# Rebuilding the last stage of a decoder block on one core: split gate weights and expert rows added in flight

## What is computed

```python
# 64 experts, 8 of them for each token; the shared expert is added to h earlier
h = h + sum over the token's 8 experts of weight * ((silu(xb @ w_gate[e]) * (xb @ w_up[e])) @ w_down[e])
h = h + (p @ w_ple) * sigmoid(rmsnorm(h, g_ple) @ w_ple_gate)     # p 512x256, w_ple 256x1024, w_ple_gate 1024x1024
out = rmsnorm(h, g_final)                                         # rmsnorm(x, g) = x * rsqrt(mean(x*x) + 1e-6) * g
```

## Time and profile before

| | |
|---|---|
| median of 3 runs | 1379.09 us (1377.03 to 1379.1) |
| the profiled execution's own time | 1374.77 us |
| its span on the core | 1373.1 us |
| PE busy over the span | 1276.9 us (93%) |
| DVE busy | 892.3 us (65%) |
| ACT busy | 580.4 us (42%) |
| POOL busy | 318.4 us (23%) |
| moved from and to HBM | 302.30 MB and 37.75 MB |

### The profile page before, as it was taken

How to read it: one execution, slowest core, us unless ns; L and a number is a source line. 1 busy time by engine, 2 the same in 40 slices (tenths; PEclk the granted TensorE clock), 3 DMA queues, 4 the chain that set the end, 5 groups by cost and what they waited for, 6 DMA issues and landing times. The chain is left out here.

```text
span 1373.1 us, 19307 instructions
## 1 busy us (share of the span) xinstructions
PE 1276.9 (93%) x6173; PEld 913.8 (67%) x6174; DVE 892.3 (65%) x1834; ACT 580.4 (42%) x943; POOL 318.4 (23%) x245
## 2 busy tenths in 40 slices
PE   4999999999999899859999999999999999997886
PEld 3777877667668795346777777777767777774333
DVE  5444244655556436667788787787887887882685
ACT  3232424343445201045655655656656556552211
POOL 5633243223224300012211221222122122211000
PEclk8999999999899999979999999999999999998799
DMA  8832122111124121279999999999999999985940
GB/s 251 228 73 57 38 62 63 46 47 48 31 55 141 29 101 53 77 281 334 359 351 357 369 359 365 357 351 363 354 357 365 364 369 360 357 314 182 426 193 31
DMA packets 123408, 306.14 MB, mean 223 GB/s; under 512 B 27328, under 2 KB 85344, under 8 KB 97632
## 3 DMA queue, kind: packets, MB, share of 16 engines
q1 hardware_dynamic: 104496, 271.38, 55.4%
q0 software_dynamic: 18864, 34.12, 6.5%
HBM read 302.30 MB, written 37.75 MB: 248 GB/s over the span
## 5 line engine op out<-in xcount | busy, mean ns | idle before, releaser
L1271 PE MATMUL bank<-sb_w_hl,sb_xgT_hl 128*128 128x512 f32 x1536 | 369.0, 396 | 6.6 <-DVE sb_xgT_hl L1405 6.6
L1271 PEld LDWEIGHTS bank<-sb_w_hl,sb_xgT_hl 128*128 128x128 f32 x1536 | 286.4, 190 | 64.1 <-DVE sb_xgT_hl L1405 6.8
L1284 PE MATMUL bank<-sb_y,sb_work 128*128 128x512 f32 x512 | 235.4, 602 | 0.9 <-ACT sb_work L1474 0.9
L195 PE MATMUL bank<-sb_x_hl,sb_w_hl 128*128 128x512 f32 x912 | 222.3, 400 | 0.0
L195 PEld LDWEIGHTS bank<-sb_x_hl,sb_w_hl 128*128 128x128 f32 x912 | 172.0, 192 | 46.4 <-issue 10.1
L1398 DVE TENSOR_TENSOR sb_w_hl<-sb_r,sb_w_hl 128x2048 fp32r<-128x2048 f32 x64 | 143.8, 2288 | 43.2 <-ACT sb_w_hl L1444 43.2
L1398 DVE TENSOR_TENSOR sb_w_hl<-sb_work,sb_w_hl 128x2048 fp32r<-128x2048 f32 x64 | 143.8, 2289 | 38.7 <-ACT sb_w_hl L1444 38.7
L1284 PEld LDWEIGHTS bank<-sb_y,sb_work 128*128 128x128 f32 x512 | 92.1, 190 | 93.0 <-issue 91.8
L869 POOL DMA_INDIRECT sb_r<-xn_rows,sb_work x66 | 68.7, 1041 | 357.2 <-PE bank L1263 276.6
L188 POOL TENSOR_TENSOR sb_w_hl<-sb_r,sb_w_hl 128x1024 fp32r<-128x1024 f32 x54 | 129.7, 2405 | 69.2 <-ACT sb_w_hl L1035 58.4
L735 ACT ACTIVATE sb_h<-sb_h,sb_small 128x31 f32<-128x31 f32 (+4 forms) x128 | 57.3, 495 | 207.9 <-DVE sb_small L642 139.2
(11 more groups left out here) (213 smaller groups left out, 1459.1 us busy)
## 6 DMA issues: line engine op xcount, KB each, us to landing
sb_y<-in_w_down SPq DMA_DIRECT2D x64, 1024.0 KB, 9.1
sb_r<-in_w_gate SPq DMA_DIRECT2D x32, 1024.0 KB, 6.9
sb_r<-in_w_up SPq DMA_DIRECT2D x32, 1024.0 KB, 8.4
sb_work<-in_w_gate SPq DMA_DIRECT2D x32, 1024.0 KB, 6.9
sb_work<-in_w_up SPq DMA_DIRECT2D x32, 1024.0 KB, 8.5
sb_r<-in_w_in SPq DMA_DIRECT2D x34, 512.0 KB, 3.9
sb_rows_even<-expert_rows SPq DMA_DIRECT2D x4, 2048.0 KB, 15.1
sb_rows_odd<-expert_rows SPq DMA_DIRECT2D x4, 2048.0 KB, 18.3
```

Of the source, the lines that this page charges most:

```text
L195: last = nc.tensor.matmul(out, w_hl[:, slot, zw, k, :], x_hl[:, zx, k, :], start=n == 0, stop=n == 3 * KD - 1)
L1271: last = nc.tensor.matmul(bank[BH][:, :], xgT_hl[:, zx, k, :], w[:, zw, :, k, :], start=n == 0, stop=n == 3 * KD - 1)
L1284: last = nc.tensor.matmul(bank[BO[i]][:, :], hT[:, c, :], wd[:, c, i * 512:(i + 1) * 512], start=c == 0, stop=c == 1)
```

## The change

The overflow block and the tail become one block. It does the following:

1. `w_ple_gate` is loaded in eight pieces of 512 KB during experts 52 to 59, one behind each expert's loads on SP's queue; for this the last twelve turns of SP's loop are written out. `g_ple` is loaded as a column per slice (`gcol`) and no longer as a broadcast row.
2. At the end of the expert block ACT scales each slice of the gate weight with the gain and rounds it (`scaled_gate_hi`), DVE forms the remainder (`scaled_gate_lo`): eight instructions of 128x1024 on each. The transposes of `p` and their two copies move there too.
3. SP loads only the first four rows of each token (2 MB per tile), into three buffers. POOL issues the second four rows as a transfer that adds them to what the buffer holds, when the first four have landed. DVE's adds are three per tile where there were six.
4. The gate product has three fp32r passes, 48 matmuls a tile. The tile is transposed unscaled, straight from `h`; ACT rounds it and DVE takes the remainder. The norm factor goes into the sigmoid's scale; ACT forms the sum of squares. The four gates have a buffer each.
5. DVE runs all four `finish` behind the last tile's remainder, and `scale_out(t-1)` behind `finish(t)`.

```diff
+                for e in range(NE - 12, NE - 2):
+                    next_gate_up(e + 2, e % 2)
+                    next_down(e, e % 2)
+                    k = e - NE + 12
+                    if k < KD:
+                        sp.dma_start(wgp[:, k], chunks(a["w_ple_gate"][0])[:, k]).then_inc(s_tail, 16)
...
                 run(dve, step)
+                dve.wait_ge(s_tail, 16 * KD)
+                for k in range(2):
+                    scaled_gate_lo(dve, k)
                 rows_out(NE - 1, 1, NE // 2 - 1)
+                for k in range(2, KD):
+                    scaled_gate_lo(dve, k)
...
+                all_rows_written(sp)
+                for t in range(NT):
+                    if t == 3:
+                        sp.wait_ge(T["added"], 1)
+                    sp.dma_start(row_at[t % 3], half_of_rows(t, 0)).then_inc(s_rows[t % 3], 16)
...
+                def add_other_half(t):
+                    pool.wait_ge(s_rows[t % 3], 16 * (t // 3) + 16)
+                    pool.dma_start(row_at[t % 3], half_of_rows(t, 1), accum_op=ALU.add, max_dma_last_dim=8192).then_inc(s_added_rows[t], 16)
...
+                    pe.wait_ge(T["xt_lo"], 2 * t + 2)
...
+                    for i in range(2):
+                        n = 0
+                        for k in range(KD):
+                            for zx, zw in PASSES:
+                                last = nc.tensor.matmul(bank[2 + 2 * (t % 2) + i][:, :], xnT_hl[:, zx, k, :],
+                                                        wg_hl[:, zw, k, i * 512:(i + 1) * 512], start=n == 0, stop=n == 3 * KD - 1)
+                                n += 1
+                        last.then_inc(T["gate_pe"], 1)
...
+                def round_rows(t):
+                    if t:
+                        act.wait_ge(T["gate_pe"], 2 * t)
+                    for i in range(2):
+                        act.wait_ge(T["xt_pe"], 2 * t + i + 1)
+                        nc.scalar.copy(xnT_hl[:, 0, 4 * i:4 * i + 4, :], psv(i, 4, P)).then_inc(T["xt_hi"], 1)
+                    squares(t, 0, 0, "ms")
...
+                round_rows(0)
+                for t in range(1, NT):
+                    gates(t - 1)
+                    round_rows(t)
+                gates(NT - 1)
...
+                def add_rows(t):
+                    rows = row_at[t % 3]
+                    dve.wait_ge(s_added_rows[t], 16)
...
+                add_rows(0)
+                for t in range(1, NT):
+                    add_rows(t)
+                    rest_of_rows(t - 1)
+                rest_of_rows(NT - 1)
+                dve.wait_ge(T["emb"], 8)
+                dve.wait_ge(s_gp, 16)
+                finish(0)
+                for t in range(1, NT):
+                    finish(t)
+                    scale_out(t - 1)
+                scale_out(NT - 1)
```

More of the change, by code:

```diff
@@ L1390, in _ @@
                 down(NE - 1, 1, NE // 2 - 1)
+                pe.wait_ge(s_p, 48)
+                pe.wait_ge(E["idx"], NE + NPAD - 1)
+                for c in range(2):
+                    for t in range(NT):
+                        last = nc.tensor.transpose(bank[(BL, 7)[c]][:, t * P:(t + 1) * P], prow[:, t, c * P:(c + 1) * P], ident)
+                    last.then_inc(T["p_tp"], 1)
             @block.vector
@@ L1531, in _ @@
                         pe.wait_ge(V["down"], 16 * j + 16)
-                        down_products(pe, Wd[0], V)
+                        down_products(pe, Wd_more, V)
                         pe.wait_ge(V["o_act"], j + 1)
+                pe.wait_ge(T["p_tc"], 2)
+                for t in range(NT):
+                    if t >= 2:
+                        pe.wait_ge(T["emb"], 2 * (t - 1))
+                    for i in range(2):
+                        for c in range(2):
+                            last = nc.tensor.matmul(bank[2 + 2 * (t % 2) + i][:, :], pTt[:, c, t * P:(t + 1) * P],
+                                                    wpl[c][:, i * 512:(i + 1) * 512], start=c == 0, stop=c == 1)
+                        last.then_inc(T["emb_pe"], 1)
@@ new lines, in _, with squares, gates @@
+            @block.scalar
+            def _(act):
+                more = act.value_load(ntot[0:1, 0:1], min_val=0, max_val=NOV)
+                with act.If(more > 0):
+                    with act.Fori(0, more) as j:
+                        act.wait_ge(V["gu"], j + 1)
+                        nc.scalar.activation(hid, bank[BH][:, 0:EH], ACT.Silu).then_inc(V["silu"], 1)
+                        act.wait_ge(V["hid"], j + 1)
+                all_rows_written(act)
+                for t in range(NT):
+                    for i in range(2):
+                        act.wait_ge(T["emb_pe"], 2 * t + i + 1)
+                        nc.scalar.copy(y[:, t, i * 512:(i + 1) * 512], bank[2 + 2 * (t % 2) + i][:, :]).then_inc(T["emb"], 1)
+                def squares(t, out, first, name):
+                    nc.scalar.activation(junk, h[:, t, :], ACT.Square, scale=D ** -0.5,
+                                         accum_out=part[:, first + t:first + t + 1]).then_inc(T[name], 1)
+                def round_rows(t):
+                    if t:
+                        act.wait_ge(T["gate_pe"], 2 * t)
+                    for i in range(2):
+                        act.wait_ge(T["xt_pe"], 2 * t + i + 1)
+                        nc.scalar.copy(xnT_hl[:, 0, 4 * i:4 * i + 4, :], psv(i, 4, P)).then_inc(T["xt_hi"], 1)
+                    squares(t, 0, 0, "ms")
+                def gates(t):
+                    act.wait_ge(T["rr"], t + 1)
+                    for i in range(2):
+                        act.wait_ge(T["gate_pe"], 2 * t + i + 1)
+                        nc.scalar.activation(sigs[t][:, i * 512:(i + 1) * 512], bank[2 + 2 * (t % 2) + i][:, :], ACT.Sigmoid,
+                                             scale=part[:, 4 + t:5 + t]).then_inc(T["sig"], 1)
+                round_rows(0)
[3 more added lines that the diff above has]
+                gates(NT - 1)
@@ L1560, in _ @@
                         dve.wait_ge(V["stored"], 16 * j + 16)
[L1562 to L1572, removed]
```

209 lines of the change are left out of this document (85 added, 124 removed).

## The result

The changed kernel takes 1399.65 us (median of 4 runs, 1395.83 to 1403.86), the kernel before 1379.09 us (1377.03 to 1379.3). The ratio is 1.0153, 95% interval 1.0122 to 1.0184: 20.6 us slower, where 11 us were forecast. The profiled execution took 1400.21 us with a span of 1398.4.

What follows compares the result with a forecast made beforehand. The tail was taken as bound first by a transfer, then by PE and DVE in turn. 1308.2 + 6.35 + 45.3 + 24.3 = 1384.1 against 1373.1, 11.0 us more, added to the median 1379.09: 1390 us, range 1375 to 1402.

Steps and rivals of the forecast that it cites:

- threefold cost: Rival for the tail's row transfers: adding costs three times a copy (15.6 us), time 1405; chance 0.13.
- 1, to SP's first row load: End of expert block: it ends later, so SP issues the first rows at about 1269.7, 2.9 us later.
- Link 2: Tail, loads until tile 1's rows are complete, at 1308.2, with 9.7 us per adding transfer, twice a plain one.
- 3, to tile 0's product: Tail, from tile 1's rows complete to the first gate product: three adds and two remainders, 6.35 us.
- Link 4: Tail, gate products: from the first product's start to tile 3's, 45.3 us, with hand-overs of 2.7 us.
- X: The start of tile 3's gate product in the tail, put 45.3 us after the first product's start.
- Link 5: Tail after tile 3's product starts: DVE's four finishes and four scalings end last, together 24.3 us.
- Waits for A2 and A3 don't bind: Tail: later tiles' row waits don't delay products; all eight transfers end by 1331.1, tile 2's product can start at 1345.8.
- the rival to which I gave 0.08: Expert stage: the cover for the extra gate weight loads fails, 3 to 7 us on top, 1393 to 1397; chance 0.08.
- Adding as fast as copying: Rival for the tail's row transfers: tile 1's rows complete at 1297.2, no change, 1379; chance 0.15.
- Served ahead of tile 2's plain load: Rival in the tail: POOL's transfers go first at a copy's rate, 4.8 us less, 1374; chance 0.14.
- A1: The time when tile 1's rows are complete in the tail, forecast at 1308.2.

Runs made afterwards that it cites:

- Experiment 1: The changed kernel with POOL's four row transfers copying and not adding, so the first four expert rows of each token are left out of the sum: 1382.57 us.
- Experiment 2: The changed kernel with the drain on POOL ahead of the root replaced by a wait on a semaphore: 1390.37 us.
- experiment 5: The kernel before with the gate weights loaded early in eight pieces, without the 4 MB load in the tail, nothing else changed: 1376.09 us.
- experiment 6: The changed kernel with the eight gate weight pieces behind every third expert from 36 on, not behind each from 52 on: 1398.28 us.
- experiment 8: The kernel of experiment 7 with the gate weight pieces spread as in experiment 6: 1367.14 us.
- experiment 9: The kernel of experiment 8 with tile 2's third half added earlier, the finishes of tiles 1 and 2 behind the last remainder, POOL's last output roots later: 1361.67 us.
- experiment 4: The changed kernel with the edits of Experiment 2 and experiment 3, and each tile's last steps put between the tiles' sums: 1380.4 us.
- experiment 7: The kernel of experiment 4 without adding transfers: SP loads all eight half tiles plainly and VectorE adds both halves: 1369.39 us.
- experiment 3: The changed kernel with VectorE forming each tile's remainder directly behind the sum of its rows: 1400.14 us.

## Why the prediction was right, and where its size was off

The direction and the mechanism hold: the adding transfers run at half rate and the tail gets longer for it. The size does not hold as well: 11.0 us were forecast and 20.6 measured. The median lies outside the 1384 to 1396 that the forecast gave "if its mechanism holds", and inside 1375 to 1402 because that range was stretched towards the threefold cost, which is not what happened. That much is luck. The chain's links, tail counted from the last group of 24 products (1244.26 before, 1253.51 after):

| link | predicted, us | measured, us | from |
|---|---|---|---|
| 1, to SP's first row load | 25.4 | 25.3 | 1253.51 to 1278.84 |
| 2, to tile 1's rows complete | 38.5 | 39.1 | to 1317.93, DVE's L1718 at 1317.95 |
| 3, to tile 0's product | 6.35 | 6.2 | to 1324.10 |
| 4, to tile 3's product, X | 45.3 | 50.5 | to 1374.64 |
| 5, to the end | 24.3 | 23.8 | to 1398.4 |
| tail | 139.9 | 144.9 | |

**Link 2** is right to 0.6 us with 9.7 us for an adding transfer. Experiment 1 shows that it is the adding. The sentence taken from the Trainium skill ("Collectives: The Full Stack", section "The bandwidth ceiling: the fold count and why AG ≠ RS ≠ AR") held for a transfer within one core as well: 215 GB/s against 426.

**Link 4** is the step that failed, by 5.2 us. The prediction said "Waits for A2 and A3 don't bind" and let the second sigmoid follow the product at once. It checked what DVE and PE wait for, and not that the sigmoid's scale comes from POOL, whose drain stands behind four adding transfers. The last row transfer did bind, by way of a root of 128 numbers. The prediction had its end nearly right (61.4 us after the first row load; measured 63.0, 1278.84 to 1341.8). Experiment 2 puts the cost at 7.4 us of tail. Without the drain the link is 43.1 us, 2.2 below the forecast: the three hand-overs take 2.57 us each, not 2.7, and the first product 13.0 and not 14.4. So an error in the other direction hid part of it.

**Link 5** is right: DVE's list ends last and has no gap of note.

```profile
1373.30 1.29 DVE L1727 TENSOR_TENSOR sb_xn3T_hl<-bank,sb_xn3T_hl 128x512 fp32r<-128x512 f32 x2 [12.47 <-ACT sb_xn3T_hl L1672]
...
1394.02 1.28 DVE L1742 SCALAR_TENSOR_TENSOR sb_h<-sb_h,sb_small,sb_r 128x1024 f32<-128x1024 f32 x1 [0.44 <-POOL sb_small L1595]
```

**The eight pieces**, which the prediction cost "at nothing", cost 3.8 us: the rival to which I gave 0.08. What failed is the size of the backlog, not the room. The room was 7.4 us for a down weight (before, issued at 1193.44 and used at 1209.94, 16.5 us later, with 9.1 to land), near the 7 of the prediction. The backlog was put at 4 to 5 us, and up to 3 for `gcol`. The down weight issued at 1198.95 landed 18.0 us later, so at the last expert it was 8.9 us. The demand of 413 GB/s (362 + 51) met 388 GB/s at a share of 1.00, which by my estimate alone is 2.0 MB, 5 us, over the 81 us. Experiments 5 and 6 show that the pieces cause it and that their density matters. Where the other 4 us come from, and why one wait of 0.7 to 1.4 us stays when the pieces are spread (0.89, 0.67 and 1.36 us in experiments 6, 8 and 9), I leave open. `gcol` was not taken away by itself in the changed kernel; in these three it is loaded sixteen experts earlier, and in experiment 5, which waits too, there is none.

**The rivals.** *Adding as fast as copying* and *threefold cost* are both excluded by the rates. *Served ahead of tile 2's plain load*: not seen, and A1 came 0.6 us late, not 16 us early. The sum of links and stage is 11.0 + 5.0 + 3.8 = 19.8 us, against 20.6 of the medians.

**What the change was worth in parts.** Early gate weights: some 2 us of gain (experiment 5, 0.15%). Adding transfers in place of plain loads, all else equal: 11 us of loss (experiments 4 and 7, 1380.4 and 1369.39). The drain: 9 us by the medians. The orders on DVE and POOL that experiment 4 mends on top of the drain: 10 us (1390.37 to 1380.4). Of that, experiment 3 alone shows nothing while the drain is there, so the two can't be valued apart. The twelve adds that DVE was spared (19 us of its time) were worth less than the transfers lost: with plain loads most of them lie beside PE's products and the transfers. Not all do: in experiment 7 the third and the fourth product start 5.0 and 4.8 us behind the end of the one before (1320.96 to 1325.97, 1338.60 to 1343.39), where the hand-over takes 2.6.

## What to carry to other kernels

Let a transfer add only where the transfer engines have time to spare: it costs them twice a copy, while the adds it saves may lie beside other work. Ask of every drain what else its engine has issued: on POOL, with a transfer in flight, it was a wait for that transfer, where a semaphore on the one result took 0.34 us. And when a stage gets a new engine order, follow the small operands too (a scale, a root), for they tie the path to an engine that looks idle.

## What the runs showed of the hardware that was not expected

- A drain on POOL held until the transfer in flight, POOL's own, had landed: 13.81 us for an adding one, 8.46 us for a plain one, with the root 0.3 us behind the landing each time (1341.8 and 1342.08, 1321.4 and 1321.71). With nothing in flight 0.15 us lie between the two instructions around it (1361.35 to 1361.51 in the changed kernel). With a semaphore in its place the root came 0.34 us behind the sum (1326.82 to 1327.16) while the transfer was in flight.
- An adding transfer from HBM into SBUF in fp32 moves 215 to 221 GB/s at a DMA share of 1.03 to 1.06; the same transfer as a copy 401 to 434 GB/s at 0.96 to 1.04 (experiment 1, 1297 to 1301).
- Near the full rate a little more load made loads land much later: with 413 GB/s wanted and 388 carried, a gate load's time to land went from 6.9 to 12.7 us, and the last down weight's from 9.1 to 18.0 us. It stays high with less: at 376 GB/s and a share of 0.97 in experiment 6 a gate load took 15.1 us, against 361 GB/s and 0.95 before.
- POOL's root over 128x1 takes 0.57 us where DVE is idle and 1.52 us in the three rows at the end of the tail that start 0.16 us behind a scaling of 1.28 us on DVE. DVE's last scaling waits for the last of them:

```profile
1392.46 1.52 POOL L1595 TENSOR_TENSOR sb_small<-sb_small,sb_cst 128x1 f32<-128x1 f32 x1 [3.52 <-DVE sb_small L214]
```
